# Keys and values of eight attention heads moved into the stage that multiplies with seven products, and its first products reordered

## The chip, the cores and the metric

The kernel runs on one core of one Trainium2 chip, in one launch. The metric is the device time of that core in microseconds (us), less is better. Engines are named as in the profile: PE is TensorE (PEld its weight load), DVE is VectorE, ACT is ScalarE, POOL is GpSimd, SP is SyncE, which issues all transfers here.

## The reference, cut to what matters

Two blocks run one after the other on a 1024 x 1024 activation (sequence by width). The change touches only the second one, after its state space branch:

```python
h = _rmsnorm(x, norm_w) * (1.0 + scale[:, None, :]) + shift[:, None, :]
proj = jnp.einsum("bsd,de->bse", h, w_in)
z_ssm, xbc, dt_raw, q, k, v, z_att, f_logit, g_logit = jnp.split(proj, offsets, axis=-1)
y_ssm = _ssd_branch(z_ssm, xbc, dt_raw, conv_w, conv_b, dt_bias, a_log, d_skip, ssm_norm_w)
y_att = _fox_branch(q, k, v, z_att, f_logit, b_f)
g_ssm, g_att = jnp.split(jax.nn.sigmoid(g_logit + b_gate), N_BRANCHES, axis=-1)
merged = g_ssm * jnp.einsum("bse,ed->bsd", y_ssm, w_proj_ssm) + g_att * jnp.einsum("bse,ed->bsd", y_att, w_proj_att)
...
# _fox_branch: eight heads of 128, causal, blocks of 128 queries
logits = jnp.einsum("bhqd,bhkd->bhqk", qi, k).astype(jnp.float32) * scale
logits = logits + fi[..., :, None] - f_cum[..., None, :]
logits = jnp.where(pi[:, None] >= kpos[None, :], logits, -jnp.inf)
probs = jax.nn.softmax(logits, axis=-1).astype(v.dtype)
return jnp.einsum("bhqk,bhkd->bhqd", probs, v)
```

So `q`, `k`, `v`, `z_att` and the gates are all products of the same `h` with columns of `w_in`, 128 columns for each head and each of `q`, `k`, `v`.

## The kernel before, in words

Everything is kept transposed: a tile has 128 features as partitions and the 1024 positions as columns, in two halves of 512. Float32 operands are split into a high part, rounded to the matmul's type, and a low part, the rest; a product takes three matmuls (high by high, high by low, low by high: `mm3`). `h` lies in SBUF split, as `Uh` and `Ul`.

**A block in the plain way** (`lin`) is 128 columns of weights by one half of 512 positions: 8 steps of 128 over the inner dimension of 1024, three matmuls each, 24 matmuls of 512 columns. A block has two halves. Its weights come by one transfer of 512 KB (`w_load`), ACT rounds them (`w_hi`, line 327), POOL subtracts (`w_lo`, line 334).

**The stage with seven products** (`stage_seven`) takes two blocks of weights at once, a pair. It treats the weights as 2 x 2 blocks (two blocks of columns by two halves of the inner dimension) and `h` as 2 x 2 (two halves of the inner dimension by two halves of positions) and forms the product with 7 multiplications in place of 8 (`PRODUCTS`: P1, P2, P7, P6, P4, P3, P5), of 12 matmuls each. So a pair takes 84 matmuls where the plain way takes 96. `SEVEN` lists the pairs, nine before: the attention's `z` (`fz`), seven of the gates `gs` and three of the gates `ga`. DVE adds weight blocks (`weight_add`), ACT and POOL split the sum (`weight_hi`, line 2684, `weight_lo`, line 2690) into one of four slots, DVE adds up the results from PSUM (`add`), ACT applies the gate, and SP stores the finished half in DRAM (`zd`, `md`, `gd`). `ORDER` is the order of the products. The sums of quadrants of `h` that P7, P6, P4 and P5 need (`quadrant`, `combine`, `x_hi`, `x_lo`) are made once, beside the first two pairs, and so the first 14 products are interleaved: P1, P2, P7 of pair 0, the same of pair 1, then P6, P4, P3, P5 of both.

**The attention** (`stage_attn_c`) is written as one loop over 64 steps, step i being block b = i % 8 (128 queries by (b + 1) x 128 keys) of head h = i // 8. In step i PE does, in this order: on odd steps the product of probabilities and values for two blocks (`values`), the transposes of block i - 3 (`turn_p`: as many as the block has key blocks, 1 to 8, line 3012), the scores of block i (`scores`), in steps 3 and 4 of a head the transposes of the values (`turn_v`), and then one piece of the projections of the **next** head (`head`): the two halves of `q` in steps 0 and 1, of `k` in 2 and 3, of `v` in 4 and 5, and a small one for the forget gate in 6 and 7. In head 7 steps 0 to 3 hold two blocks of `ga` instead and steps 4 to 7 hold nothing. Head 0's projections stand ahead of the loop.

What ties the engines together in a step: the transposed probabilities go to PSUM banks 4 and 5, one set for all blocks; ACT rounds them (line 3048), DVE takes the low part (line 3135), and only then may PE write the next transposes. The first `values` of a head waits for the low part of the transposed values (DVE, line 3157), which waits for ACT's rounding of them (line 3068).

The engines run their own queues in program order, and wait for each other by semaphores. The raw weights have two buffers, the halves of results of `stage_seven` six.

Of the kernel before, what the change touches and what calls it, by code (L numbers as in the profile page):

```python
# [11 lines left out]
P = 128  # L12
# [21 lines left out]
SEVEN = [(("fz", n), ("fz", n + 1)) for n in range(0, 8, 2)] + [(("gs", n), ("gs", n + 1)) for n in range(1, 7, 2)] + [  # L34
# [9 lines left out]
def weight_plan():  # L44
# [67 lines left out]
    first = {"fz": Z_ATT, "gs": G_LOG, "ga": G_LOG + 1024}  # L112
# [78 lines left out]
def program(nc, io, table):  # L191
    xT, pT, wflat, wada, vecs, rows, cst, abias, tabs, out = io
    stack = ExitStack()
    with stack:
# [50 lines left out]
        gd = nc.dram_tensor("gd", (8, P, T), F32, kind="Internal").ap()  # L245

# [2265 lines left out]
        def stage_ssm_out():  # L2512
# [70 lines left out]
            def gpsimd():  # L2583
# [7 lines left out]
                for n in range(8):  # L2591
                    w_lo(po, PSM[n] + 2)
                    if n == 6:
                        for x in range(2):
                            weight_lo(x)
                on.ends(po, "end ssm", "po")

            def sync():
                w_load(GS + 4)
                for n in range(8):  # L2600
                    w_load(PSM[n] + 4)
                    for hf in range(2):
# [31 lines left out]
        ORDER = [(p, q) for q in ("P1", "P2", "P7") for p in (0,)] + [(1, "P1"), (1, "P2"), (1, "P7")]  # L2634
        ORDER += [(p, q) for q in PRODUCTS[3:] for p in range(2)] + [(p, q) for p in range(2, len(SEVEN)) for q in PRODUCTS]
# [85 lines left out]
        def stage_seven():  # L2721
# [55 lines left out]
            def scalar():  # L2777
                for x in range(2, 4):
                    weight_hi(x)
                for j in range(2):  # L2780
                    x_hi("P6", j)
                    ac.activation(two(kept, j), two(fl["P6"], j), ACT.Copy).then_inc(*on.up(ac, "seven_ac/keep", j))
                for x, (p, q) in enumerate(ORDER):
# [4 lines left out]
                    if x == 1:  # L2788
                        for j in range(2):
                            x_hi("P4", j)  # L2790
                    if x == 4:
                        for j in range(2):
                            x_hi("P5", j)
# [6 lines left out]
            def add(p, q):  # L2800
                what = ps[:, bank[p, q], :]
                u, v_ = tile[p, 0, 1], tile[p, 1, 1]
                if q == "P1":
                    return
# [7 lines left out]
                elif q == "P6":  # L2812
# [5 lines left out]
                    dv.tensor_tensor(v_, ps[:, bank[p, "P7"], :], u, ALU.add).then_inc(*on.up(dv, "seven_dv/read", p, "P7"))  # L2818
                elif q == "P4":
# [5 lines left out]
                elif q == "P3":  # L2825
                    on.wait_ge(dv, "seven_dv/read", p, "P7")
                    dv.tensor_tensor(u, what, u, ALU.add).then_inc(*on.up(dv, "seven_dv/read", p, q))
                elif q == "P5":
# [4 lines left out]
                    on.ends(dv, "seven_dv/out", p, 0, 1)  # L2833

# [7 lines left out]
            def vector():  # L2842
                on.wait_ge(dv, "end ssm", "pe")
                for j in range(2):
# [4 lines left out]
                    combine("P6", j, fl["P6"], fh["P6"], ALU.add)  # L2849
                for x, (p, q) in enumerate(ORDER):  # L2850
                    if x + 5 < len(ORDER):
                        weight_add(*ORDER[x + 5])
                    if x == 0:
                        for j in range(2):
                            x_lo("P6", j)
                    add(p, q)
                    if x in (1, 4):
                        to = {1: "P4", 4: "P5"}[x]
                        for j in range(2):
                            quadrant((1, int(x == 4)), j, to, fl)  # L2860
# [18 lines left out]
            def sync():  # L2879
                pair_load(1)  # L2880
# [11 lines left out]
            def store(p, r, hf):  # L2892
                nm, n = SEVEN[p][r]
                on.wait_ge(sp, "seven_ac/gate", p, r, hf)
                if nm == "gs":
                    on.wait_ge(sp, "seven_dv/gated", p, r, hf)
                to = {"fz": zd, "gs": md, "ga": gd}[nm]
# [17 lines left out]
            return [stored[y][-1] for y in range(6)]  # L2915

        tiles_stored = stage_seven()
# [4 lines left out]
        Kf = [(Y([P, T], F32R), Y([P, T], F32R)) for _ in range(2)]  # L2922
        Vfh, Vfl = Y([P, 8, P], F32R), Y([P, 8, P], F32R)
# [10 lines left out]
        def stage_attn_c():  # L2934
            FQ, FK, FV, GA = BLK["fq"], BLK["fk"], BLK["fv"], BLK["ga"]
            NF = 64
            parts = [(FQ, 0), (FQ, 1), (FK, 0), (FK, 1), (FV, 0), (FV, 1), None, None]
# [41 lines left out]
            def head(h, s, b):  # L2979
                if parts[s]:  # L2980
                    W, hf = parts[s]
                    frees = {id(FQ): [("fq_lo", h, hf)], id(FK): [("fk_lo", h, hf)], id(FV): [("vf", h, hf)]}[id(W)]
                    bank[W[h], hf] = lin(W[h], hf, b, Uh, Ul, need_c, frees)
                else:
                    hf = s - 6
# [29 lines left out]
            def turn_v(h, c):  # L3015
                wait_bank(5)
                on.wait_ge(pe, "vf", h, c)
# [16 lines left out]
            def scalar():  # L3034
                for event in tiles_stored:
                    on.wait_ge(ac, *event)
                for s in range(8):
                    head_ac(0, s)
                    if s in (0, 2):
                        w_hi(parts[s][0][0] + 2)  # L3040
                w_hi(FV[0] + 2)
                for i in range(NF + 4):
# [15 lines left out]
                    if i and head_step(i - 1) and (i - 1) % 8 in (1, 3, 5):  # L3058

                        w_hi(parts[(i - 1) % 8][0][(i - 1) // 8 + 1] + 2)  # L3060
# [31 lines left out]
            def head_ac(h, s):  # L3092
                if parts[s]:
                    W, hf = parts[s]
# [386 lines left out]
```

## Time and profile before

| | |
|---|---|
| median of three runs | 2838.76 us (2838.16 to 2839.21) |
| the profiled execution | 2831.54 us, span 2830.2 us |
| PE busy, share of the span | 97% |
| DVE, ACT, POOL busy | 60%, 49%, 32% |
| chain that ended last | PE 89%, DVE 4%, ACT 3%, POOL 2% |
| PE's share of the chain in `mm3` (line 343) | 83% |
| HBM read, written | 139.10 MB, 26.21 MB |

The span is from the first to the last instruction of the profiled execution. A busy share is an average over stages with different limits; "idle before" in brackets in a row is the time an engine stood still ahead of the instruction, with what ended it. The seven-product stage runs from about 1954 us to 2141 us of the span, the attention from there to about 2640 us (with some blocks of `ga` at its end).

### The profile page before, as it was taken

Reading aid. Unit: us, or ns where it says so; the run is one execution under the profiler, and the core shown is the slowest. Engines: PE = TensorE matmul, PEld = TensorE weight load, DVE = VectorE, ACT = ScalarE, POOL = GpSimd, SP = SyncE. Lnnn points to the kernel's source line nnn. Section 1 sums busy time; section 2 is a strip of 40 time slices with the busy share of each in tenths; the row PEclk is TensorE's granted clock in tenths of the full one; section 3 lists DMA queues with packets and bytes.
Section 4 is the critical chain, followed back from the end, with each engine's and each line's share of the span. In section 5 each row is a group of like instructions: output and inputs, shape, how many; then the busy total and the mean of one; then the engine's idle time right before and its main releaser. Section 6 shows DMA issues by size and latency. Waiting matters only on the chain.

```text
span 2830.2 us, 36562 instructions
## 1 busy us (share of the span) xinstructions
PE 2737.2 (97%) x13692; PEld 2249.9 (79%) x13692; DVE 1684.0 (60%) x2861; ACT 1387.1 (49%) x2550; POOL 908.0 (32%) x745
## 2 busy tenths in 40 slices
PE   8999989999999999999998999998999999999997
PEld 6778867777788888887876777776787888888876
DVE  6667775643278888887557874556552444443344
ACT  5767863434266767675346335542432343334222
POOL 0334441223365655562122221123541111111431
PEclk9999999999999999999999999999999999999999
DMA  3111131221100000003211310033342110111242
GB/s 135 41 31 42 36 124 68 91 83 38 39 10 13 10 11 10 11 31 112 73 47 36 112 38 23 23 126 104 115 146 99 37 36 24 30 30 31 82 149 75
DMA packets 62367, 167.68 MB, mean 59 GB/s; under 512 B 7024, under 2 KB 15856, under 8 KB 61040
## 3 DMA queue, kind: packets, MB, share of 16 engines
q1 hardware_dynamic: 62192, 165.34, 17.7%
q8 instruction: 111, 1.82, 0.3%
q14 instruction: 64, 0.52, 0.1%
HBM read 139.10 MB, written 26.21 MB: 58 GB/s over the span
## 4 chain that ended last, share of the span: by engine, by line
PE 89%; DVE 4%; ACT 3%; POOL 2%; issue 2%; DMA 0%; POOLq 0%; ACTq 0%; DVEq 0%
PE ps L343 83%; PE ps L461 4%; PE ps L3012 1%; PE ps L787 1%; POOL t L1779 0%; POOL t L1327 0%; POOL t L1331 0%; ACT t L327 0%; DVE t L3370 0%; DMA t<-in_wflat 0%; DVE t L2337 0%; DVE t L1906 0%; DVE t L563 0%; ACT t L826 0%; POOL t L1329 0%
## 5 line engine op out<-in xcount | busy, mean ns | idle before, releaser
L343 PE MATMUL ps<-t,t 128*128 128x512 f32 (+8 forms) x11804 | 2579.0, 377 | 68.7 <-POOL t L2690 10.9
L343 PEld LDWEIGHTS ps<-t,t 128*128 128x128 f32 (+4 forms) x11804 | 2048.5, 185 | 528.9 <-issue 68.5
L334 POOL TENSOR_TENSOR t<-t,t 128x1024 fp32r<-128x1024 f32 (+2 forms) x151 | 322.6, 2137 | 1131.2 <-ACT t L327 769.4
L327 ACT ACTIVATE t<-t 128x1024 fp32r<-128x1024 f32 (+2 forms) x187 | 167.8, 898 | 437.5 <-PE ps L343 437.1
L1719 DVE TENSOR_TENSOR t<-ps,t 128x512 fp32r<-128x512 f32 x256 | 164.6, 684 | 33.3 <-ACT t L1627 31.2
L1779 POOL TENSOR_SCALAR t<-t,t 128x1024 f32<-128x1024 f32 x128 | 143.6, 1122 | 119.3 <-DVE t L1725 114.3
L461 PE MATMUL ps<-t,t 128*128 128x128 f32 x1176 | 157.4, 274 | 11.5 <-POOL t L1779 9.2
L461 PEld LDWEIGHTS ps<-t,t 128*128 128x128 f32 x1176 | 132.7, 141 | 30.2 <-issue 14.4
L1732 DVE TENSOR_REDUCE t<-ps 128x1 f32<-128x1024 f32 x128 | 154.2, 1204 | 0.5 <-PE ps L343 0.5
L1635 ACT ACTIVATE t<-ps,t 128x1024 f32<-128x1024 f32 x128 | 142.9, 1117 | 3.5 <-DVE t L1732 3.3
L1627 ACT ACTIVATE t<-ps 128x512 fp32r<-128x512 f32 x256 | 139.0, 591 | 9.4 <-PE ps L461 5.5
L2690 POOL TENSOR_TENSOR t<-t,t 128x512 fp32r<-128x512 f32 x63 | 90.1, 1436 | 89.0 <-ACT t L2684 89.0
L965 POOL TENSOR_SCALAR t<-t,t 128x384 f32<-128x384 f32 (+1 forms) x128 | 69.2, 560 | 129.1 <-DVE t L912 129.1
L1266 POOL TENSOR_TENSOR t<-t,t 128x512 f32<-128x512 f32 x31 | 49.6, 1600 | 147.3 <-DVE t L1175 147.3
L3135 DVE TENSOR_TENSOR t<-ps,t 128x128 fp32r<-128x128 f32 (+3 forms) x64 | 48.4, 756 | 74.8 <-ACT t L3048 74.7
L2684 ACT ACTIVATE t<-t 128x512 fp32r<-128x512 f32 x63 | 39.0, 627 | 79.7 <-PE ps L343 45.2
L826 ACT ACTIVATE t<-t,t 128x384 f32<-128x384 f32 (+1 forms) x128 | 73.8, 579 | 3.3 <-DVE t L896 2.8
L1327 POOL TENSOR_TENSOR t<-t,t 32x512 f32<-32x512 f32 x34 | 43.6, 1282 | 75.8 <-DVE t L1322 75.5
L3048 ACT ACTIVATE t<-ps 128x128 fp32r<-128x128 f32 (+3 forms) x64 | 41.7, 652 | 50.5 <-PE ps L3012 50.5
L2473 ACT ACTIVATE t<-ps,t 128x128 f32<-128x128 f32 x128 | 34.8, 383 | 60.1 <-PE ps L343 53.9
L887 DVE CUSTOM_DVE_ANT_0 t<-ps,t 128x384 f32<-128x384 f32 (+1 forms) x128 | 61.3, 519 | 4.1 <-PE ps L343 3.3
L334 DVE TENSOR_TENSOR t<-t,t 128x1024 fp32r<-128x1024 f32 (+1 forms) x36 | 31.6, 879 | 49.5 <-ACT t L327 49.5
(245 smaller groups left out, 2537.6 us busy)
## 6 DMA issues: line engine op xcount, KB each, us to landing
t<-in_wflat SPq DMA_DIRECT2D x138, 512.0 KB, 3.6
t<-in_wada SPq DMA_DIRECT2D x48, 256.0 KB, 4.9
t<-in_wflat SPq DMA_DIRECT2D x9, 1024.0 KB, 5.9
t<-in_xT SPq DMA_DIRECT2D x16, 512.0 KB, 7.2
md<-t SPq DMA_DIRECT2D x30, 256.0 KB, 3.2
t<-md SPq DMA_DIRECT2D x30, 256.0 KB, 4.0
t<-in_wflat SPq DMA_DIRECT2D x32, 128.0 KB, 2.0
hd<-t SPq DMA_DIRECT2D x8, 512.0 KB, 3.1
```

Source lines behind the costliest of these rows:

```text
L327: ac.activation(parts(i)[0][:, 0:n], raw[i % 2][:, 0:n], ACT.Copy).then_inc(*on.up(ac, "whi", i))
L334: e.tensor_tensor(lo[:, 0:n], raw[i % 2][:, 0:n], hi[:, 0:n], ALU.subtract) \
L343: return pe.matmul(o, l, r, start=start, stop=stop)
L461: t = pe.transpose(o[:, c * P:(c + 1) * P], src[:, c * P:(c + 1) * P], ident)
L826: ac.activation(S[:, r, 0:nk], S[:, r, 0:nk], ACT.Exp, bias=M[:, 8 + r:9 + r], accum_out=M[:, 16 + r:17 + r]) \
L965: po.tensor_scalar(S[:, r, 0:nk], S[:, r, 0:nk], M[:, 20 + r:21 + r], 1.0, ALU.mult, ALU.mult).then_inc(*on.up(po, "a probs", i, r))
L1627: ac.activation(to, src, ACT.Copy).then_inc(*on.up(ac, "b pT_hi", i - 3, c))
L1635: ac.activation(Pm[u][:, :], o, ACT.Exp, bias=bm[:, c0:c0 + 1], accum_out=bm[:, c0 + 1:c0 + 2]).then_inc(*on.up(ac, "b exp", i - 1))
L1719: dv.tensor_tensor(to, src, turned(i - 3, c, 0)[0], ALU.subtract).then_inc(*on.up(dv, "b pT_lo", i - 3, c))
L1732: dv.tensor_reduce(bm[:, c0:c0 + 1], o, AX, ALU.max, negate=True).then_inc(*on.up(dv, "b max", i))
L1779: po.tensor_scalar(Pm[u][:, :], Pm[u][:, :], bm[:, c0 + 2:c0 + 3], 1.0, ALU.mult, ALU.mult).then_inc(*on.up(po, "b probs", i - 1))
L2690: po.tensor_tensor(lo[:, :, :], weight(p, W_QUAD[q]), hi[:, :, :], ALU.subtract).then_inc(*on.up(po, "seven_po", p, q))
```

## The change

`SEVEN` gets eight more pairs at its front, (`fk`, h) with (`fv`, h): the keys and the values of head h. The blocks `fk` and `fv` leave the plain way. Their results go to two new DRAM tensors, `kd` and `vd`, without a gate, and come back in the attention by one transfer each per head (`key_load` into `Kraw`, which shares its place with the low part of the keys; `value_load` into `Vf`). ACT and DVE split the keys from SBUF instead of PSUM, and the copy of the values from PSUM by ACT goes away. In the attention, `q` of the next head stands in steps 0 and 3, the split of its keys in 1 and 2, and steps 4 and 5 have no projection.

`ORDER` puts P3 of pairs 0 and 1 directly behind their P7, and the DVE, ACT and SP code of the first 14 products is placed anew for it.

```diff
-SEVEN = [(("fz", n), ("fz", n + 1)) for n in range(0, 8, 2)] + ...
+SEVEN = [(("fk", h), ("fv", h)) for h in range(8)] + [(("fz", n), ("fz", n + 1)) for n in range(0, 8, 2)] + ...
...
     for h in range(8):
-        for nm, c in (("fq", Q_ATT), ("fk", K_ATT), ("fv", V_ATT)):
-            add(nm, W, None, 1024, (c + 128 * h, c + 128 * h + 128))
+        add("fq", W, None, 1024, (Q_ATT + 128 * h, Q_ATT + 128 * h + 128))
...
                 for n in range(8):
                     w_load(PSM[n] + 4)
+                    if n == 7:
+                        pair_load(1)
...
-        ORDER = [(p, q) for q in ("P1", "P2", "P7") for p in (0,)] + [(1, "P1"), (1, "P2"), (1, "P7")]
-        ORDER += [(p, q) for q in PRODUCTS[3:] for p in range(2)] + [(p, q) for p in range(2, len(SEVEN)) for q in PRODUCTS]
+        ORDER = [(p, q) for p in range(2) for q in ("P1", "P2", "P7", "P3")] + [(p, q) for q in ("P6", "P4", "P5") for p in range(2)]
+        ORDER += [(p, q) for p in range(2, len(SEVEN)) for q in PRODUCTS]
...
+                if nm in ("fk", "fv"):
+                    return
                 on.wait_ge(ac, "seven_dv/out", p, r, hf)
...
-                for x in range(2, 4):
-                    weight_hi(x)
+                weight_hi(2)
                 for j in range(2):
                     x_hi("P6", j)
                     ac.activation(two(kept, j), two(fl["P6"], j), ACT.Copy).then_inc(*on.up(ac, "seven_ac/keep", j))
+                    if j == 0:
+                        weight_hi(3)
...
-            parts = [(FQ, 0), (FQ, 1), (FK, 0), (FK, 1), (FV, 0), (FV, 1), None, None]
+            query = {0: 0, 3: 1}
+            key = {1: 0, 2: 1}
+            forget = {6: 0, 7: 1}
...
             def turn_v(h, c):
                 wait_bank(5)
-                on.wait_ge(pe, "vf", h, c)
+                on.wait_ge(pe, "m4", "v", h)
...
+                elif s in key:
+                    hf = key[s]
+                    for ev in slot_free(h):
+                        on.wait_ge(ac, *ev)
+                    on.wait_ge(ac, f"m{h % 2}", "k", h)
+                    ac.activation(Kf[h % 2][0][:, half(hf)], Kraw[h % 2][:, half(hf)], ACT.Copy).then_inc(*on.up(ac, "fk_hi", h, hf))
...
+            def key_load(h):
+                for ev in slot_free(h):
+                    on.wait_ge(sp, *ev)
+                for event in kept_at["fk", h]:
+                    on.wait_ge(sp, *event)
+                sp.dma_start(Kraw[h % 2][:, :], kd[h]).then_inc(*on.landed(sp, f"m{h % 2}", "k", h))
+
+            def value_load(h):
+                if h:
+                    on.wait_ge(sp, "c vT", h - 1, 1)
+                for event in kept_at["fv", h]:
+                    on.wait_ge(sp, *event)
+                sp.dma_start(Vf[:, :], vd[h]).then_inc(*on.landed(sp, "m4", "v", h))
```

Two places show what moves. The first is PE's queue in step 4 of head 0. In the kernel before it holds, after two transposes of probabilities, the scores of 640 keys, the transposes of the values' second half (line 461), and then a plain block. Of the two operands the moving one stands first: the keys (t_23367, t_23368) ahead of the queries, `h` (t_70, t_71) ahead of the block's weights (t_52, t_54):

```order
L3012 MATMUL ps<-t_55,t_23377 128x128 [waits s_probs_dv,s_pT_lo,s_pT_hi]
L3012 MATMUL ps<-t_55,t_23377 128x128
L343 MATMUL ps<-t_23367,t_23363 128x512 [waits s_fq_lo,s_max]
L343 MATMUL ps<-t_23368,t_23363 128x512
L343 MATMUL ps<-t_23367,t_23364 128x512
L343 MATMUL ps<-t_23367,t_23363 128x128
L343 MATMUL ps<-t_23368,t_23363 128x128
L343 MATMUL ps<-t_23367,t_23364 128x128
L343 MATMUL ps<-t_57,t_56 128x128
L461 MATMUL ps<-t_55,t_23378 128x128 [waits s_v_lo,s_v_hi]
L461 MATMUL ps<-t_55,t_23378 128x128 x3
L343 MATMUL ps<-t_70,t_52 128x512 [waits s_fk_lo,s_wlo_po,s_whi]
```

The same place in the changed kernel, from the scores of the last 128 keys on; t_24725 and t_24726 are the high and low part of the transposed probabilities, t_24723 and t_24724 those of the transposed values:

```order
L344 MATMUL ps<-t_24717,t_24714 128x128
L344 MATMUL ps<-t_57,t_56 128x128
L462 MATMUL ps<-t_55,t_24730 128x128 [waits s_v_lo,s_v_hi]
L462 MATMUL ps<-t_55,t_24730 128x128 x3
L344 MATMUL ps<-t_24725,t_24723 128x256 [waits s_v_lo,s_pT_lo,s_og]
L344 MATMUL ps<-t_24726,t_24723 128x256
L344 MATMUL ps<-t_24725,t_24724 128x256
```

Behind the transposes of the values there now stands at once the product with the values, which waits for their low part (s_v_lo); the 24 matmuls between the two are gone.

The second is ACT's queue at the start of the seven-product stage. t_20790, t_20792, t_20796 and t_20798 are the high parts of the four weight slots, t_20794 and t_20795 the raw weights of pairs 0 and 1, t_20778 and t_20781 the operand of P6 and its sum, t_20788 the copy that is kept. Before:

```order
L2684 ACTIVATE t_20796<-t_20794 128x512 [waits s_seven_dv]
L2684 ACTIVATE t_20798<-t_20795 128x512 [waits s_w71]
L2710 ACTIVATE t_20778<-t_20781 128x1024 [waits s_seven_dv]
L2782 ACTIVATE t_20788<-t_20781 128x1024
L2710 ACTIVATE t_20778<-t_20781 128x1024 [waits s_seven_dv]
L2782 ACTIVATE t_20788<-t_20781 128x1024
L2764 ACTIVATE t_63<-ps 128x512 [waits s_md2,s_md3,s_md1,s_ssm,s_md0,s_mm]
```

And in the changed kernel:

```order
L2688 ACTIVATE t_20796<-t_20794 128x512 [waits s_seven_dv]
L2714 ACTIVATE t_20778<-t_20781 128x1024 [waits s_seven_dv]
L2787 ACTIVATE t_20788<-t_20781 128x1024
L2688 ACTIVATE t_20798<-t_20794 128x512 [waits s_seven_dv]
L2714 ACTIVATE t_20778<-t_20781 128x1024 [waits s_seven_dv]
L2787 ACTIVATE t_20788<-t_20781 128x1024
L2768 ACTIVATE t_63<-ps 128x512 [waits s_md2,s_md3,s_md1,s_ssm,s_md0,s_mm]
L2688 ACTIVATE t_20790<-t_20795 128x512 [waits s_w71]
```

The fourth slot now takes a block of pair 0 (P3) and waits for DVE, not for the transfer of pair 1 (s_w71); the first weights of pair 1 have moved behind both halves of P6's operand and the first copy out of PSUM (line 2768).

## Rows read from the trace of the kernel before

**Rows 1.** Windows (us): busy time (x count) by engine, granted PE clock, DMA share, GB/s.

```profile
1955.00:1990.00 35.00, 24.09 (x85) 18.20 (x85) 29.57 (x23) 13.56 (x18) 15.25 (x8) 0.85 0.22 82
2180.00:2560.00 380.00, 379.27 (x2056) 321.57 (x2055) 159.61 (x408) 145.41 (x304) 51.34 (x22) 1.00 0.13 42
2580.00:2593.00 13.00, 10.00 (x66) 8.54 (x64) 8.83 (x23) 7.39 (x14) 2.37 (x1) 1.00 0.14 42
```

**Rows 2.** Timeline of DVE, end of the seven-product stage (start us, us, what).

```profile
2127.77 0.69 DVE L2810 TENSOR_TENSOR t<-ps,t 128x512 f32<-128x512 f32 x1 [2.11 <-PE ps L343]
...
2141.37 0.69 DVE L2830 TENSOR_TENSOR t<-ps,t 128x512 f32<-128x512 f32 x1 [2.03 <-PE ps L343]
```

**Rows 3.** Timeline of ACT, plain blocks of head 0 ahead of the loop.

```profile
2147.05 0.60 ACT L3105 ACTIVATE t<-ps 128x512 fp32r<-128x512 f32 x1 [3.62 <-PE ps L343]
...
2174.96 0.60 ACT L3100 ACTIVATE t<-ps 128x512 f32<-128x512 f32 x1 [5.00 <-PE ps L343]
```

**Rows 4.** Timeline of PE, one middle head of the attention.

```profile
2357.51 0.30 PE L3012 MATMUL ps<-t,t 128*128 128x128 f32 x1
...
2364.45 0.38 PE L3012 MATMUL ps<-t,t 128*128 128x128 f32 x2
...
2385.59 0.84 PE L3012 MATMUL ps<-t,t 128*128 128x128 f32 x6
...
2394.69 0.95 PE L3012 MATMUL ps<-t,t 128*128 128x128 f32 x7
...
2401.55 1.04 PE L3012 MATMUL ps<-t,t 128*128 128x128 f32 x8
2402.34 9.28 PE L343 MATMUL ps<-t,t 128*128 128x384 f32 x52
2411.45 0.30 PE L3012 MATMUL ps<-t,t 128*128 128x128 f32 x1
```

**Rows 5.** Timeline, head 7, steps 4 to the end of 7.

```profile
2580.20 0.38 PE L3012 MATMUL ps<-t,t 128*128 128x128 f32 x2
...
2583.53 0.69 DVE L3157 TENSOR_TENSOR t<-ps,t 128x512 fp32r<-128x512 f32 x1 [0.19 <-ACT t L3068]
2584.37 0.88 PE L343 MATMUL ps<-t,t 128*128 128x256 f32 x6 [2.23 <-DVE t L3157]
...
2593.18 0.85 PE L3012 MATMUL ps<-t,t 128*128 128x128 f32 x6 [0.26 <-issue]
```

**Rows 6.** Timeline, the last transposes of the attention and what follows on ACT and DVE.

```profile
2601.53 0.95 PE L3012 MATMUL ps<-t,t 128*128 128x128 f32 x7
...
2602.51 0.92 ACT L3048 ACTIVATE t<-ps 128x896 fp32r<-128x896 f32 x1 [6.52 <-PE ps L3012]
2603.47 1.09 DVE L3135 TENSOR_TENSOR t<-ps,t 128x896 fp32r<-128x896 f32 x1 [1.32 <-ACT t L3048]
...
2609.14 1.01 ACT L3048 ACTIVATE t<-ps 128x1024 fp32r<-128x1024 f32 x1
...
2610.18 1.23 DVE L3135 TENSOR_TENSOR t<-ps,t 128x1024 fp32r<-128x1024 f32 x1 [5.62 <-ACT t L3048]
```

**Rows 7.** Waits of PE: total us, times, longest.

```profile
PE ps L343 <- POOL t L2690: 10.9, 4, 5.0
```

**Rows 8.** Timeline, start of the seven-product stage.

```profile
1959.28 0.49 SPq L2645 DMA_DIRECT2D t<-in_wflat  x1
...
1966.16 0.63 ACT L2684 ACTIVATE t<-t 128x512 fp32r<-128x512 f32 x1 [10.67 <-DMA t<-in_wflat]
...
1968.19 4.61 PE L343 MATMUL ps<-t,t 128*128 128x512 f32 x12 [4.98 <-POOL t L2690]
...
1983.54 16.81 PE L343 MATMUL ps<-t,t 128*128 128x512 f32 x62 [4.71 <-POOL t L2690]
```

**Rows 9.** DMA issues of the page: count, KB each, us to landing.

```profile
t<-in_wflat SPq DMA_DIRECT2D x138, 512.0 KB, 3.6
...
t<-in_wflat SPq DMA_DIRECT2D x9, 1024.0 KB, 5.9
```

More of the change, by code:

```diff
@@ L31 @@
 X_ORDER = [0, 1, 2, 3, 8, 9, 4, 5, 6, 7]
-SEVEN = [(("fz", n), ("fz", n + 1)) for n in range(0, 8, 2)] + [(("gs", n), ("gs", n + 1)) for n in range(1, 7, 2)] + [
+SEVEN = [(("fk", h), ("fv", h)) for h in range(8)] + [(("fz", n), ("fz", n + 1)) for n in range(0, 8, 2)] + [(("gs", n), ("gs", n + 1)) for n in range(1, 7, 2)] + [
     (("gs", 7), ("ga", 5)), (("ga", 6), ("ga", 7))]
@@ L2787, in scalar @@
                         weight_hi(x + 4)
-                    if x == 1:
+                    if x in (3, 6):
                         for j in range(2):
[L2790 to L2793, printed above, removed]
+                            x_hi("P4" if x == 3 else "P5", j)
                     for _, p_, r, hf in [o for o in outs if o[0] == x - 1]:
@@ L2802, in add @@
                 u, v_ = tile[p, 0, 1], tile[p, 1, 1]
-                if q == "P1":
+                if q == "P1" or q == "P3" and p < 2:
                     return
@@ L2818, in add @@
                     dv.tensor_tensor(v_, ps[:, bank[p, "P7"], :], u, ALU.add).then_inc(*on.up(dv, "seven_dv/read", p, "P7"))
+                    if p < 2:
+                        third(p)
                 elif q == "P4":
@@ L2825, in add @@
                 elif q == "P3":
-                    on.wait_ge(dv, "seven_dv/read", p, "P7")
-                    dv.tensor_tensor(u, what, u, ALU.add).then_inc(*on.up(dv, "seven_dv/read", p, q))
+                    third(p)
                 elif q == "P5":
@@ L2833, in add, with third @@
                     on.ends(dv, "seven_dv/out", p, 0, 1)
+            def third(p):
+                u = tile[p, 0, 1]
+                on.wait_ge(dv, "mm/seven", p, "P3")
+                on.wait_ge(dv, "seven_dv/read", p, "P7")
+                dv.tensor_tensor(u, ps[:, bank[p, "P3"], :], u, ALU.add).then_inc(*on.up(dv, "seven_dv/read", p, "P3"))
             def scale(p, r, hf):
@@ L2893, in store @@
                 nm, n = SEVEN[p][r]
-                on.wait_ge(sp, "seven_ac/gate", p, r, hf)
+                if nm in ("fk", "fv"):
+                    on.wait_ge(sp, "seven_dv/out", p, r, hf)
+                else:
+                    on.wait_ge(sp, "seven_ac/gate", p, r, hf)
                 if nm == "gs":
                     on.wait_ge(sp, "seven_dv/gated", p, r, hf)
-                to = {"fz": zd, "gs": md, "ga": gd}[nm]
+                to = {"fk": kd, "fv": vd, "fz": zd, "gs": md, "ga": gd}[nm]
                 sp.dma_start(to[n, :, half(hf)], tile[p, r, hf]).then_inc(*on.landed(sp, f"pt{store_of[p, r, hf]}", p, r, hf))
@@ L2914, in stage_seven @@
             sync()
-            return [stored[y][-1] for y in range(6)]
-        tiles_stored = stage_seven()
+            kept_at = {SEVEN[p][r]: [(f"pt{store_of[p, r, hf]}", p, r, hf) for hf in range(2)] for p in range(len(SEVEN)) for r in range(2)}
+            return [stored[y][-1] for y in range(6)], kept_at
+        tiles_stored, kept_at = stage_seven()
         Y = region(YO)
@@ L2922, in program @@
         Kf = [(Y([P, T], F32R), Y([P, T], F32R)) for _ in range(2)]
+        Kraw = [at(YO + 16384 + 8192 * x + 4096, [P, T]) for x in range(2)]
         Vfh, Vfl = Y([P, 8, P], F32R), Y([P, 8, P], F32R)
@@ L2979, in head @@
             def head(h, s, b):
[L2980 to L2985, printed above, removed]
+                if s in query:
+                    hf = query[s]
+                    bank[FQ[h], hf] = lin(FQ[h], hf, b, Uh, Ul, need_c, [("fq_lo", h, hf)])
+                elif s in forget:
+                    hf = forget[s]
                     bank["f", h, hf] = b
@@ L3038, in scalar @@
                     head_ac(0, s)
[L3039 to L3041 removed]
+                    if s == 3:
+                        w_hi(FQ[0] + 2)
                 for i in range(NF + 4):
@@ L3057, in scalar @@
                             .then_inc(*on.up(ac, "c exp", i - 1))
-                    if i and head_step(i - 1) and (i - 1) % 8 in (1, 3, 5):
-                        w_hi(parts[(i - 1) % 8][0][(i - 1) // 8 + 1] + 2)
+                    if i and head_step(i - 1) and (i - 1) % 8 == 3:
+                        w_hi(FQ[(i - 1) // 8 + 1] + 2)
                     if i in (NF - 6, NF - 4):
```

99 lines of the change are left out of this document (52 added, 47 removed).

## The prediction

> **What bounds the kernel now.** I read the windows first, then PE's own timeline, then who waited. The windows show that the attention is bound by PE: of 380 us PE is busy for 379.27, DVE for 159.61, ACT for 145.41 [rows 1]. A matmul taken out there shortens the run for as long as PE stays the engine that is never waited for. The seven-product stage has PE waits only at its start: four, 10.9 us together, all for POOL's low weight parts [rows 7]; at the full rate of its steady part it waits for nothing.
>
> Then the price of the two ways to compute a block. In the steady part of the seven-product stage DVE is released by the end of a product at 2127.77 and at 2141.37, five products later: 2.72 us a product [rows 2]. In the plain way ACT is released at 2147.05 and at 2174.96, five half blocks later: 5.58 us each [rows 3]. A pair costs 7 x 2.72 = 19.0 us one way and 4 x 5.58 = 22.3 us the other.
>
> Third, what the plain blocks hide. A middle head takes PE from 2357.51 to 2411.45 (one transpose to the next single transpose), 53.9 us, with no idle time [rows 4]; six half blocks are 33.5 of them. In head 7, steps 4 to 7 have no block behind them, and there PE does stand still: 2.23 us for the low part of the values on DVE, itself released by ACT [rows 5]. The changed kernel makes that the state of every head.
>
> **The change, part by part.**
>
> *Products added.* 8 pairs x 7 = 56 products x 2.72 = +152.3 us. The added pairs need no gate on ACT, DVE's and POOL's work per pair is as before, and PE waited for none of them in the steady part.
>
> *Half blocks removed.* 8 heads x 4 = 32 x 5.58 = -178.6 us, if PE never waits. Together -26.3 us. That is what the edit gives on paper.
>
> *Cover lost in steps 4 to 7, heads 0 to 6.* From the two transposes of step 4 to the six of the next step 0 a middle head takes 2385.59 - 2364.45 = 21.14 us [rows 4]. Two half blocks less: 9.98. Head 7 does the same work without blocks, and takes 2593.18 - 2580.20 = 12.98 [rows 5]. So 3.0 us are waits. Two small matmuls for the forget gate come on top in heads 0 to 6; they partly fall into the waits, so I take 3.2 (bounds 2.3, the one named wait, and 3.6). What is late: step 4 transposes the values, ACT takes them behind a transposed block, an exponential and a rounding of weights, DVE behind that, and the product with the values stands right behind it in PE's queue (first place of the queues above). 7 x 3.2 = +22.4 us.
>
> *Cover lost in steps 1 and 2, heads 1 to 6.* Before, the seven transposes of step 1, the eight of step 2 and the product with the values in step 3 each had a half block between them. All transposes share banks 4 and 5, so the next may start only when ACT and DVE have read the last. The last head shows the pieces. Seven transposes: 0.95 on PE, 0.92 on ACT, 1.09 on DVE, with the hops between them 3.07 us until the eight may start. Eight: 1.04 + 1.01 + 1.23, with hops 3.4 until the product with the values may start [rows 4, 6]. That product and what goes with it take 9.11 (2402.34 to 2411.45) less a half block of 5.58 less the scores, 0.58 (three matmuls of 384 columns at 5.58 / 24 per 512, and the mask) = 2.95 [rows 4]. In all 3.07 + 3.41 + 2.95 = 9.4 us from the seven transposes to the single one. PE's own work there is 2411.45 - 2394.69 = 16.76 less two half blocks = 5.6. So 3.8 us of waits (bounds 3.3 and 4.4 for the hops), x 6 = +23 us. The split of the keys, now from SBUF, stands behind the transposed block on ACT and DVE, and delays neither.
>
> *Start of the attention.* Head 0 loses the cover in steps 1 and 2 too, where its first transpose waits for the first exponential, and ACT takes a rounding of weights ahead of the forget gate. No row has it; it lies between nothing and the half block that hid it, 5.6. I take +3.
>
> *First keys and values.* A reload of 512 KB takes 3.6 us to land [rows 9]. It is issued when the scores of the head before last in that buffer are done (end of step 7) and read in step 1 of the next head, with a half block of 5.58 and 3 us of other PE work between: hidden. Without that cover it would cost up to 3.6 us a head.
>
> *Reordered first products.* PE waits 4.98 us ahead of 1968.19 for pair 1, whose transfer is issued at 1959.28 and lands by 1966.16, and 4.71 us ahead of 1983.54 [rows 8]. P3 of pair 0 needs no transfer and fills 2.7 us of the first wait; P3 of pair 1 fills the same of the second. The slow clock goes too: the 12 matmuls at 1968.19 take 4.61 us instead of 2.72, the 62 at 1983.54 take 16.81 instead of 14.1, and the clock of the stretch is 0.85 [rows 1, 8]. Against it: pair 1's first weights stand on ACT behind both halves of P6's operand (second place of the queues), about a product later; and pair 2's transfer, 5.9 us [rows 9], starts after P5 of pair 0 as before, while the 14 products now end sooner, so PE may wait for it. I take -6 us, between 0 and -15 (all of the waits and some 4 us of slow clock).
>
> **The sum**: -26.3 + 22.4 + 23 + 3 - 6 = +16 us. The profiled execution took 2831.54, so 2847.6 in its terms; the median of the runs lies 7.2 above it, so I forecast 2838.8 + 16 = 2855 us, +0.57%.
>
> **The rivals.**
>
> *PE's clock falls in every head* (slower by far). After a wait of 5 us the 12 matmuls took 4.61 us [rows 8]. Were it so after the waits of each head, two groups of that size at 1.9 us for 7 heads would add 27 us: 2882. Against it: head 7 has 3 us of idle time in 13 at a granted clock of 1.00, 2.4 GHz [rows 1], and the new waits are no longer, 1.8 to 2.5 us, though they recur. The Trainium skill ("TensorE: Matmul & The Clock Gate", HAM oscillation) describes a loop in which every round waits, the clock falls in the wait, and each round starts at the low rate. By that rule the time would be the 2882; by head 7's row it stays at the forecast. 8%.
>
> *The second pair of waits isn't there* (faster). If the transposes of steps 1 and 2 did not bind, 23 us go: -7, 2832. The place is the read of banks 4 and 5 by line 3135. It decides where waits in the attention fall below 32 us in all. For it speaks only that no row has such a wait, as a block always covered it; against it the durations in [rows 6], each measured. 9%.
>
> *Waits a third smaller, or all of the start's 15 us recovered*: within 0.2% of before, 2835 to 2844. 9%.
>
> *Reloads late*: SP's queue is one, and a key transfer stands behind weights and the `z` tiles. 7 heads x 2 us: 2869. 5%.
>
> *The start gives nothing*, since the weights only wait elsewhere: 2861 to 2864. 7%.
>
> The forecast's own case, 2846 to 2862, gets 62%.
>
> **How the numbers follow.** 0.2%, 5.7 us, is about what a measurement of this kernel can tell from no change. Slower: 62 + 8 + 5 + 7 = 82%; same 9; faster 9. The bounds of the terms give 7 x 2.3 + 6 x 3.3 - 15 - 26.3 = -5 at one end and 7 x 3.6 + 6 x 4.4 + 5.6 - 26.3 = +31 at the other; the range from 2839 to 2869 leaves out the faster case below and the clock above.
>
> **What would show it.** In the changed profile: the seven-product stage is longer by 152 less some 6 us, with 2.7 us a product; PE's waits at its start fall from 10.9 to about 5. A middle head takes 53.9 - 22.3 + 7.0 = 38.6 us from single transpose to single transpose. PE waits on the values' low part (line 3157 before) some 2.3 us in seven heads more, and on the transposed low part (line 3135 before) some 3.8 us a head. The clock in the attention stays 1.00. It is wrong if a head takes near 32 us (no waits) or over 42 (clock or reloads), or if the stage's start grows.

## The result, and the profile after

The changed kernel takes 2870.41 us (median of 4 runs, 2864.94 to 2872.38), the kernel before 2838.66 us on the same chip (4 runs, 2838.16 to 2839.21). The ratio is 1.0115, 95% interval 1.0101 to 1.0129: slower, as forecast, but 15 us above the forecast of 2855 and just outside the range that ended at 2869. The profiled execution took 2868.45 us with a span of 2867.0, the one before 2831.54 with 2830.2. Between the profiles lie 36.8 us of span, between the medians 31.8; the sum of the prediction was +16. The account below goes by the profiles, so it has 20.8 us to explain, and not the 15.4 of the medians.

The page's first part for the kernel after, and the first line of its fourth (the chain that ended last, by engine):

```profile
PE 2728.9 (95%) x13596; PEld 2243.1 (78%) x13596; DVE 1752.4 (61%) x2949; ACT 1404.0 (49%) x2582; POOL 955.5 (33%) x785
...
PE 86%; DVE 6%; ACT 3%; issue 2%; POOL 2%; DMA 0%; POOLq 0%; ACTq 0%; DVEq 0%
```

PE falls from 97% of the span to 95%, and DVE's share of the chain rises from 4% to 6%: PE now stands waiting for DVE. The waits of PE say where (total us, times, longest). Only those of the two stages that the change touches stand here:

```profile
PE ps L344 <- DVE t L3178: 17.5, 8, 2.2
PE ps L344 <- DVE t L3156: 13.0, 12, 1.9
PE ps L3037 <- issue: 10.8, 7, 1.8
...
PE ps L344 <- POOL t L2694: 7.7, 5, 2.9
...
PE ps L344 <- DVE t L2822: 7.0, 1, 7.0
...
PE ps L3037 <- DVE t L3174: 2.0, 1, 2.0
```

Line 3178 takes the low part of the transposed values, line 3156 that of the transposed probabilities (3157 and 3135 before); line 3037 is the transpose. The wait put down to "issue" is that of the eight transposes: they start at 2399.22, right behind the end of the low part of the seven, which reads the same banks 4 and 5:

```profile
2398.03 1.09 DVE L3156 TENSOR_TENSOR t<-ps,t 128x896 fp32r<-128x896 f32 x1 [1.31 <-ACT t L3072]
```

These three waits make 41 us; before, the first two of them made 2.8 us, in head 7 alone [rows 5]. The start's wait on POOL went down from 10.9 [rows 7] to 7.7, but one of 7.0 us for line 2822 is new.

PE's timeline, two middle heads in a row, from single transpose to single transpose (start us, us, what; in brackets the idle time before and what ended it):

```profile
2367.13 0.30 PE L3037 MATMUL ps<-t,t 128*128 128x128 f32 x1
...
2374.06 0.38 PE L3037 MATMUL ps<-t,t 128*128 128x128 f32 x2
...
2378.18 0.88 PE L344 MATMUL ps<-t,t 128*128 128x256 f32 x6 [2.19 <-DVE t L3178]
...
2383.12 1.59 PE L344 MATMUL ps<-t,t 128*128 128x256 f32 x12 [0.29 <-DVE t L3156]
...
2386.98 0.85 PE L3037 MATMUL ps<-t,t 128*128 128x128 f32 x6
...
2396.08 0.95 PE L3037 MATMUL ps<-t,t 128*128 128x128 f32 x7
...
2399.22 1.06 PE L3037 MATMUL ps<-t,t 128*128 128x128 f32 x8 [1.76 <-issue]
...
2402.75 4.49 PE L344 MATMUL ps<-t,t 128*128 128x256 f32 x24 [1.88 <-DVE t L3156]
2407.03 0.37 PE L3037 MATMUL ps<-t,t 128*128 128x128 f32 x1
...
2439.22 1.06 PE L3037 MATMUL ps<-t,t 128*128 128x128 f32 x8 [1.76 <-issue]
...
2442.74 3.04 PE L344 MATMUL ps<-t,t 128*128 128x256 f32 x24 [1.88 <-DVE t L3156]
2445.62 0.30 PE L3037 MATMUL ps<-t,t 128*128 128x128 f32 x1
```

The second head takes 2445.62 - 2407.03 = 38.59 us, the forecast's 38.6. The first takes 39.90 with the very same waits: the 24 matmuls of the values' product take 4.49 instead of 3.04 us. The windows of three heads give the reason in the third value from the row's end, the granted clock (the DMA share and GB/s stand behind it). The first of them goes from step 3 of head 0 to step 3 of head 1:

```profile
2324.78:2367.13 42.35, 36.41 (x198) 31.94 (x199) 24.54 (x64) 18.54 (x42) 2.37 (x1) 0.88 0.21 78
2367.13:2407.03 39.90, 33.57 (x200) 29.27 (x200) 22.71 (x58) 17.59 (x39) 2.38 (x1) 0.96 0.12 40
2407.03:2445.62 38.59, 32.24 (x200) 27.95 (x201) 22.72 (x58) 17.58 (x39) 2.38 (x1) 1.00 0.13 42
```

Within the first middle head the clock is down only behind the second pair of waits, at 2399.22 and 2402.75. Through the wait of 2.19 us at 2378.18 it stays at 1.00 (2374.00 to 2387.00):

```profile
2380.00:2390.00 10.00, 9.49 (x59) 8.05 (x58) 8.93 (x21) 8.09 (x19) 0.00 (x0) 1.00 0.33 105
2390.00:2400.00 10.00, 8.24 (x54) 7.29 (x53) 4.08 (x14) 2.44 (x6) 0.00 (x0) 1.00 0.01 2
2400.00:2410.00 10.00, 8.12 (x47) 7.53 (x46) 5.96 (x17) 3.50 (x8) 0.00 (x0) 0.83 0.00 1
```

The start of the seven-product stage on PE, and then DVE there:

```profile
1962.66 3.01 PE L344 MATMUL ps<-t,t 128*128 128x512 f32 x12 [0.91 <-POOL t L2694]
1968.59 3.06 PE L344 MATMUL ps<-t,t 128*128 128x512 f32 x12 [2.92 <-POOL t L2694]
1974.17 9.80 PE L344 MATMUL ps<-t,t 128*128 128x512 f32 x36 [2.52 <-POOL t L2694]
1984.97 3.02 PE L344 MATMUL ps<-t,t 128*128 128x512 f32 x12 [0.99 <-POOL t L2694]
1988.34 5.78 PE L344 MATMUL ps<-t,t 128*128 128x512 f32 x24 [0.35 <-POOL t L2694]
2001.12 9.05 PE L344 MATMUL ps<-t,t 128*128 128x512 f32 x32 [7.00 <-DVE t L2822]
```

```profile
1995.02 1.29 DVE L2673 TENSOR_TENSOR t<-t 128x512 f32<-128x512 f32 x2
1996.22 3.42 DVE L2720 TENSOR_TENSOR t<-t,t 128x1024 fp32r<-128x1024 f32 x2
1999.57 0.68 DVE L2818 TENSOR_TENSOR t<-ps,t 128x512 f32<-128x512 f32 x1
2000.28 0.69 DVE L2822 TENSOR_TENSOR t<-ps,t 128x512 f32<-128x512 f32 x1
```

The products go round the eight PSUM banks. The eleventh, P4 of pair 0, writes the bank of the third, P7 of pair 0. That bank is read by line 2822, which comes behind P6's add; and ahead of P6's add DVE has the weight sums and the low part of P5's operand (line 2720, 3.42 us). PE is released when line 2822 has read, at 2000.97. The banks are taken in turn, so it doesn't help that those of P1 and P2 of pair 1 have been read by then. In the order before, P6 of pair 0 was the seventh product and its adds stood ahead of that work.

**The account, by stretches.** Each starts and ends with an instruction that both kernels have. The ends of before are those of its own trace ([rows 2] has the last product's read at 2141.37). First the ends that no row has shown yet, before and after:

```profile
1960.19 3.01 PE L343 MATMUL ps<-t,t 128*128 128x512 f32 x12 [0.91 <-POOL t L2690]
2195.73 0.27 PE L3012 MATMUL ps<-t,t 128*128 128x128 f32 x1
2573.27 0.30 PE L3012 MATMUL ps<-t,t 128*128 128x128 f32 x1
```

```profile
2299.43 0.69 DVE L2835 TENSOR_TENSOR t<-ps,t 128x512 f32<-128x512 f32 x1 [2.03 <-PE ps L344]
2324.78 0.33 PE L3037 MATMUL ps<-t,t 128*128 128x128 f32 x1 [1.97 <-DVE t L3174]
2609.80 0.30 PE L3037 MATMUL ps<-t,t 128*128 128x128 f32 x1
```

| stretch | before | after | difference | forecast |
|---|---|---|---|---|
| start of the span to P7 of pair 0 | 1960.19 | 1962.66 | +2.5 | 0 |
| to the last product's read (2141.37; 2299.43) | 181.18 | 336.77 | +155.6 | +146.3 |
| to the single transpose in step 3 of head 0 | 54.36 | 25.35 | -29.0 | -30.5 |
| seven heads, to that of head 7 | 377.54 | 285.02 | -92.5 | -99.7 |
| to the end | 256.9 | 257.2 | +0.3 | 0 |

The forecast column is the terms of the sum laid on these stretches: 152.3 - 6; six half blocks and +3; 26 half blocks, 22.4 and 23. The miss of 20.8 us is 9.3 in the start, 7.2 in the seven heads, 2.5 ahead of P7 of pair 0, 1.5 at the attention's start, and 0.3 at the end.

### The profile page after: what moved, and what is told of

Read it like the earlier page. It is cut to its first block, busy times and chain, and to the rows that moved or that the text cites. A ratio compares the mean times of both kernels' runs of the same rounds, so it can differ in the third digit from the quotient of the medians.

```text
span 2867.0 us, 36671 instructions
## 1 busy us (share of the span) xinstructions
PE 2728.9 (95%) x13596; PEld 2243.1 (78%) x13596; DVE 1752.4 (61%) x2949; ACT 1404.0 (49%) x2582; POOL 955.5 (33%) x785
## 4 chain that ended last, share of the span: by engine, by line
PE 86%; DVE 6%; ACT 3%; issue 2%; POOL 2%; DMA 0%; POOLq 0%; ACTq 0%; DVEq 0%
PE ps L344 80%; PE ps L462 4%; PE ps L3037 1%; PE ps L788 1%; DVE t L3156 1%; ACT t L328 1%; POOL t L1780 0%; POOL t L1328 0%; POOL t L1332 0%; ACT t L3072 0%; DVE t L2709 0%; DVE t L3165 0%; DVE t L3409 0%; DVE t L2703 0%; DVE t L888 0%
## 5 line engine op out<-in xcount | busy, mean ns | idle before, releaser
L344 PEld LDWEIGHTS ps<-t,t 128*128 128x128 f32 (+3 forms) x11708 | 2041.9, 186 | 560.0 <-issue 98.6
L335 POOL TENSOR_TENSOR t<-t,t 128x1024 fp32r<-128x1024 f32 (+2 forms) x135 | 284.3, 2106 | 1050.6 <-ACT t L328 752.3
L328 ACT ACTIVATE t<-t 128x1024 fp32r<-128x1024 f32 (+2 forms) x171 | 151.1, 883 | 425.7 <-PE ps L344 425.6
L2694 POOL TENSOR_TENSOR t<-t,t 128x512 fp32r<-128x512 f32 x119 | 174.5, 1469 | 160.2 <-ACT t L2688 160.2
L2688 ACT ACTIVATE t<-t 128x512 fp32r<-128x512 f32 x119 | 74.5, 631 | 180.5 <-PE ps L344 130.0
L462 PEld LDWEIGHTS ps<-t,t 128*128 128x128 f32 x1176 | 133.1, 141 | 30.5 <-issue 14.6
L335 DVE TENSOR_TENSOR t<-t,t 128x1024 fp32r<-128x1024 f32 (+1 forms) x36 | 31.6, 878 | 48.7 <-ACT t L328 48.7
```

The lines of the kernel that those rows point to most:

```text
L328: ac.activation(parts(i)[0][:, 0:n], raw[i % 2][:, 0:n], ACT.Copy).then_inc(*on.up(ac, "whi", i))
L335: e.tensor_tensor(lo[:, 0:n], raw[i % 2][:, 0:n], hi[:, 0:n], ALU.subtract) \
L344: return pe.matmul(o, l, r, start=start, stop=stop)
L462: t = pe.transpose(o[:, c * P:(c + 1) * P], src[:, c * P:(c + 1) * P], ident)
L2688: ac.activation(slots[x % 4][0][:, :, :], weight(p, W_QUAD[q]), ACT.Copy).then_inc(*on.up(ac, "seven_ac/w", p, q))
L2694: po.tensor_tensor(lo[:, :, :], weight(p, W_QUAD[q]), hi[:, :, :], ALU.subtract).then_inc(*on.up(po, "seven_po", p, q))
```

## The experiments

Two questions were open: is the start's +9.3 the bank of P7, or something the eight added pairs do; and is the seven heads' loss a matter of the waits alone, or of the clock? All times are against the kernel before on the same chip: 2833.09 us there (15 runs) for the first, second and fourth experiment, 2832.83 us (7 runs) for the others. The changed kernel itself was timed only beside the kernel before at 2838.66 us, so an experiment is compared with it by the two ratios or, better, by stretches of the traces. The ratios are estimated from all the runs and can differ a little from the quotient of the medians. Every edit is to the changed kernel, where nothing else is said.

### The reordered start alone

The kernel before, with the first 14 products in the new order and their ACT, DVE, POOL and SP code, and nothing else of the change.

```diff
-        ORDER = [(p, q) for q in ("P1", "P2", "P7") for p in (0,)] + [(1, "P1"), (1, "P2"), (1, "P7")]
-        ORDER += [(p, q) for q in PRODUCTS[3:] for p in range(2)] + [(p, q) for p in range(2, len(SEVEN)) for q in PRODUCTS]
+        ORDER = [(p, q) for p in range(2) for q in ("P1", "P2", "P7", "P3")] + [(p, q) for q in ("P6", "P4", "P5") for p in range(2)]
+        ORDER += [(p, q) for p in range(2, len(SEVEN)) for q in PRODUCTS]
```

> The kernel before with only the reordered first 14 products (nine pairs as before). Theory A: 2838.7 + 3 = 2842 us, with a wait of PE of 5 to 7 us for the add of P7's result. Rival B: 2833 us, no such wait. If the wait depends on the gates that the first pairs have here and the new ones have not, it is longer than 7 us.

Measured: 2841.12 us (10 runs), ratio 1.0022 (1.0010 to 1.0034). The waits of PE in its trace:

```profile
PE ps L343 <- POOL t L2693: 7.7, 5, 2.9
...
PE ps L343 <- DVE t L2819: 7.1, 1, 7.1
```

They are the changed kernel's waits, without the new pairs. From P7 of pair 0 to the last product's read it takes 2150.65 - 1966.20 = 184.45 us, against 181.18 before: +3.3 where the sum had -6. The reorder by itself costs time. The medians differ by 8.0 us, the stretch by 3.3. The ten times lie in two groups: three from 2832.59 to 2836.62 at a mean granted clock of 0.991 to 0.994, and seven from 2841.06 to 2845.65 at 0.989 to 0.990. The profiled one is of the second group, and in it P7 of pair 0 starts 6.0 us later than in the profile of before; that part is taken up below.

### The low part of P5's operand later

DVE takes it behind the adds that free the banks of pair 0 and 1.

```diff
-                    if x in (0, 4, 7):
+                    if x in (0, 4, 10):
                         for j in range(2):
-                            x_lo({0: "P6", 4: "P4", 7: "P5"}[x], j)
+                            x_lo({0: "P6", 4: "P4", 10: "P5"}[x], j)
```

> The changed kernel with one edit: DVE makes the low part of P5's operand (two instructions, 3.4 us) after the adds of P6's results, not before. Theory A: the ninth to eleventh products wait for the PSUM bank of P7, which those adds free; the 7.0 us wait falls by 3.4 us and the time to 2867 us. Rival: P5's own operand is then late and the wait moves there; no change from 2870 us.

Measured: 2862.74 us (4 runs), ratio 1.0106 (1.0091 to 1.0122). PE at the eleventh product:

```profile
1994.77 7.56 PE L344 MATMUL ps<-t,t 128*128 128x512 f32 x25 [3.69 <-DVE t L2822]
```

The wait falls by 3.3 us, from 7.00 to 3.69, near the 3.42 us of the two instructions that moved, and no wait for P5's operand comes in its place. The stretch falls from 336.77 to 2293.17 - 1959.66 = 333.51. So DVE's queue ahead of line 2822 is what PE waited for. Of the other 3.7 us nothing was tried; P5's operand sums and the weight sums still stand ahead there. The ratios, 1.0106 and 1.0115, are too near to tell apart; it is the stretch that shows the gain.

### The old start, with the new pairs

The changed kernel with the first 14 products and their code as before; the lines of the first diff backwards.

> The changed kernel with the eight new pairs, but the first 14 products of the seven-product stage in the order and code of before. From P7 of pair 0 to the last product the stage took 181.2 us before, 184.5 us with the reordered start alone and 336.8 us in the changed kernel. Theory A (the reordered start costs 3.3 us, with or without the new pairs): here that stretch takes 333.5 us, and the time is 3 us under the changed kernel's, ratio to before near 1.010. Rival B (the prediction, the reordering gains 6 us): 343 us, ratio 1.0135.

Measured: 2863.93 us (4 runs), ratio 1.0100 (1.0081 to 1.0120). The stretch takes 2293.20 - 1959.78 = 333.42 us, 3.35 less than in the changed kernel. Its waits on POOL are those of before, and none is for a bank:

```profile
PE ps L344 <- POOL t L2691: 10.7, 4, 4.8
```

The eight pairs alone thus cost 333.42 - 181.18 = 152.24 us: the 152.3 of the sum. They add nothing to the start. The time is again told by the stretch: the ratios of 1.0100 and 1.0115 have intervals that overlap.

### The queries' blocks spread over the waits

After the change each head has two half blocks left, for the queries of the next head, in steps 0 and 3, where PE needs no cover. They are cut into pieces of 3 to 15 matmuls and put where PE waits. ACT's and DVE's parts of the queries move a step later.

```diff
-            query = {0: 0, 3: 1}
+            query = {2: 0, 4: 1}
+            pieces = {0: [(0, 0, 3)], 1: [(0, 3, 6)], 2: [(0, 6, None), (1, 0, 1)], 3: [(1, 1, 3)], 4: [(1, 3, None)]}
...
-                if s in query:
+                if h and s in pieces:
+                    for hf, k0, k1 in pieces[s]:
+                        bank[FQ[h], hf] = lin(FQ[h], hf, (7, 3)[hf], Uh, Ul, need_c, [("fq_lo", h, hf)], None, k0, k1)
+                elif s in query:
```

> The changed kernel with the two half blocks of q of the next head cut into pieces of 9 to 15 matmuls behind steps 0, 1, 2 and 4 of a head (6 in step 3), where PE waits, instead of whole blocks in steps 0 and 3. Same work. Theory A (the waits are latency of single chains, each 2 to 3 us, that any matmul can cover): a middle head falls from 39.9 us to 31.6 to 33, and the time by 7 x 7 to 7 x 8 us, to 2815 to 2823 us, below the kernel before. Rival (DVE and ACT are too far behind in a head as a whole, so that waits only move): a head stays above 36 us and the time above 2845 us.

Measured: 2824.45 us (6 runs), ratio 0.9964 (0.9952 to 0.9976): faster than before, though the start still has its 7.0 us wait. It is just above the 2815 to 2823 us expected. A middle head (line 3198 takes the low part of the queries, line 3160 that of the transposed probabilities):

```profile
2359.91 0.30 PE L3041 MATMUL ps<-t,t 128*128 128x128 f32 x1
...
2369.59 1.34 PE L344 MATMUL ps<-t,t 128*128 128x512 f32 x7 [0.53 <-DVE t L3198]
...
2373.53 1.59 PE L344 MATMUL ps<-t,t 128*128 128x256 f32 x12 [0.59 <-DVE t L3160]
...
2392.77 0.30 PE L3041 MATMUL ps<-t,t 128*128 128x128 f32 x1
```

32.86 us, where 53.94 less four half blocks of 5.58 is 31.6. The same matmuls, in another order, take 5.7 us a head less than in the 38.59 us head. All but 1.2 us of a head's loss was cover that was missing, and nothing else that the change brought: the reloads and the split from SBUF are still there.

### Both: spread blocks and the old start

> Both mended: the pieces of q behind the steps where PE waits (as in the run before) and the old start. Theory: the two are additive, the head at 32.9 us and the stretch at 333.5 us; 3.3 us less than the spread pieces alone, ratio to before near 0.995. Rival: the gain of the start is lost in the attention, ratio 0.9964 as before.

Measured: 2818.06 us (4 runs), ratio 0.9939 (0.9920 to 0.9958). The interval touches that of the spread pieces alone, so the traces must tell. From P7 of pair 0 to the last product's read it takes 2298.66 - 1965.43 = 333.23 us, where the spread pieces alone take 2303.12 - 1966.45 = 336.67, and the heads take 32.8: the two gains add up. It is the fastest kernel here that does all the work, and brings in 14.8 us of the 26.3 on paper.

### Useless matmuls in the waits

The changed kernel with 7, 7 and 9 extra matmuls of 512 columns behind steps 1, 2 and 4 of each head, whose result nobody reads. It does more work than the changed kernel; what it takes away is only that PE stands still.

```diff
                         head(*head_step(i), (7, 1, 7, 3, 7, 5, 7, 7)[i % 8])
+                        if i % 8 in (1, 2, 4):
+                            fill({1: 7, 2: 7, 4: 9}[i % 8])
...
+            def fill(n):
+                wait_bank(7)
+                for _ in range(n):
+                    mm(ps[:, 7, :], idr[:, :], Uh[:, 0, half(0)], True, True)
```

> The changed kernel with 7, 7 and 9 useless matmuls of 512 columns behind steps 1, 2 and 4 of heads 0 to 6, written to a bank that nobody reads: PE is busy in place of waiting, all other work is the same. Theory A (some 1.3 us a head are matmuls at the low clock behind the waits): the product with the values in step 3 takes 3.0 us again in place of 4.4 to 4.5, a middle head falls from 39.9 to about 38.7 us, and the time by 6 to 9 us; the granted clock in the attention is 1.00. Rival (the matmuls are slow for another reason, or the low clock costs nothing on the path): the head stays at 39.9 us or grows.

Measured: 2860.18 us (4 runs), ratio 1.0088 (1.0071 to 1.0104). The end of a middle head:

```profile
2399.92 3.04 PE L344 MATMUL ps<-t,t 128*128 128x256 f32 x24 [0.21 <-DVE t L3163]
2402.80 0.30 PE L3044 MATMUL ps<-t,t 128*128 128x128 f32 x1
```

and five heads in one window, first of the changed kernel, then of this one:

```profile
2350.00:2550.00 200.00, 168.31 (x1004) 146.23 (x1004) 114.67 (x295) 87.94 (x196) 11.90 (x5) 0.97 0.12 40
```

```profile
2350.00:2550.00 200.00, 195.62 (x1154) 165.89 (x1152) 115.47 (x293) 90.25 (x200) 11.94 (x5) 1.00 0.13 40
```

Every middle head now takes 38.5 us (2364.29, 2402.80, 2441.29), and the values' product 3.04. The seven heads take 2602.43 - 2325.82 = 276.61 us, against 285.02 in the changed kernel, whose other instructions are the same: with more matmuls 8.4 us less, at a clock of 1.00 instead of 0.97. This is the price of the clock in that trace, and 276.61 lies 1.2 us below the 377.54 - 99.7 = 277.8 of the forecast.

### Thin keys and values in the kernel before

The kernel before, where the keys' and values' blocks of heads 1 to 7 do 3 of their 24 matmuls, the rest left out. No new pairs, no reloads, no transfers changed. There is one run of it.

```diff
-                    bank[W[h], hf] = lin(W[h], hf, b, Uh, Ul, need_c, frees)
+                    bank[W[h], hf] = lin(W[h], hf, b, Uh, Ul, need_c, frees) if W is FQ or not h else thin(W[h], hf, b, frees)
```

> The kernel before with the projections of k and v of heads 1 to 7 cut to 3 matmuls of their 24 (one eighth of the inner dimension; the rest is left out), nothing else changed: no new pairs, no reloads, keys split from PSUM. It takes 28 x 21 x 0.2325 = 137 us of PE work out of the attention. Theory A (lost cover is what made PE wait, whatever the keys come from): a middle head takes 38 us or more instead of 53.94 - 4 x 4.88 = 34.4, with waits for the low parts of the values and of the transposed probabilities, and the profiled time is 2720 to 2730 us. Rival (the waits come from the reloads or the split from SBUF): the head takes 34.4 us, the time 2695 us.

Measured: 2719.32 us. Middle heads take 37.56 us (2268.10 to 2305.63 to 2343.19), 3.1 more than the 34.4 that the matmuls left need (53.94 less four times 21 of 24 parts of 5.58), with these waits:

```profile
PE ps L343 <- DVE t L3166: 13.7, 8, 2.2
...
PE ps L343 <- DVE t L3144: 7.7, 7, 1.1
```

They are the waits for the values' low part and the transposed low part again. Both numbers lie just under what was expected of my theory (38 and more, 2720 to 2730), since each thin block still covers a little and the queries' blocks stand in steps 0 and 1 here. That reason is not tested. They are far from the 34.4 and 2695 of the rival. Taking the matmuls away is enough to make the waits. The values' product takes 3.03 us here and the clock from 2350 to 2450 us is 1.00: behind waits of 1.6 and 1.1 us it did not fall.

## Why the prediction was right about the sign and short by 15 us

**The two prices held.** The old start with the new pairs shows 152.24 us for the 56 products (sum: 152.3). The half blocks were 5.58 each: the spread kernel's head of 32.86 less its waits of 0.53 and 0.59 is 31.7, where 53.94 less four half blocks is 31.6.

**Cover lost in steps 4 to 7: right.** From the two transposes of step 4 to the six of the next step 0 the changed kernel takes 2386.98 - 2374.06 = 12.92 us, with a wait of 2.19 for the values' low part and 0.29 behind it. The forecast had 9.98 + 3.2 = 13.2, from head 7 [rows 5].

**Cover lost in steps 1 and 2: right.** From the seven transposes to the eight 3.14 us (3.07), on to the values' product 3.53 (3.41), and from there to the single transpose 2445.62 - 2442.74 = 2.88 (2.95). Together 9.55 against 9.43. The chain of small durations on PE, ACT and DVE, with the hops between them [rows 6], gave a wait that no row of before showed. The rival in which these waits were absent falls.

**Reloads of keys and values: hidden, right.** At the first keys, ACT waits for a transfer once, on a place that PE does not feel:

```profile
2306.59 1.16 ACT L3128 ACTIVATE t<-t 128x512 fp32r<-128x512 f32 x2 [0.88 <-DMA t<-kd]
```

**The reordered first products: the step that failed.** The sum said "I take -6 us, between 0 and -15"; the runs show +3.3. Part of the argument came true: the wait on POOL fell by 3.2 us, from 10.9 to 7.7 and not to about 5, and the 12 matmuls behind the longest of these waits take 3.06 us, not 4.61. P3 of pair 0 "needs no transfer", but its weights are a sum that DVE makes, and it waits 2.92 us for their low part itself. Little of the slow clock was saved: behind the new wait it is 0.67 from 2001.12 to 2006.12. The waits together rise by 3.8 us and the stretch by 3.3. Without the bank's wait of 7.0 it would be some 3.7 us shorter than before, an estimate from these two numbers; no run shows it.

What turned the gain into a loss is the bank: the step looked at what PE's next operand waits for, and never at what its next bank waits for. P3 of two pairs put early means that two more banks are filled before the first read of P7's, while DVE's queue kept P5's operand ahead of that read. The step's own bounds excluded a loss, with no reason given for it. The reordered start alone shows the 3.3 us as a loss and the old start as a gain of 3.35. The later low part shows that the bank's wait hangs on DVE's queue.

**The clock: a rival that came true in part.** "PE's clock falls in every head" was given 8% and a price of 27 us, 1.9 for each of two groups of 12 matmuls a head. (The 1.9 is 4.61 less 2.72, the steady distance of two products; a group of 12 at the full clock has 3.01 in the row of 1960.19, so the same row gives 1.6.) What happened costs 8.4 us in seven heads: 3.9 in the first, where the starting waits of the attention stand close together and the clock is 0.88, and 1.4 in three of the others, where some of the 24 matmuls behind the waits of 1.76 and 1.88 us ran at the low one of the two levels, 1.2 GHz; three stayed at 1.00. The claim "The clock in the attention stays 1.00" rested on head 7 with 3 us of idle time in 13 [rows 1]. That row showed the waits of steps 4 to 7. It did not show the second pair of waits with 1.65 us of work between them (2399.22 to 2400.87), and in the middle heads the drop stands only behind that pair. So the sum had a term at nothing that measured 8.4 us. The Trainium skill ("TensorE: Matmul & The Clock Gate", HAM oscillation) describes a loop whose waits let the clock fall so that each round starts at the low rate; the trace agrees in kind, and differs in that only some rounds do. By the sum: 1.2 us fewer for the waits, 8.4 more for the clock, +7.2.

**Start of the attention: +3 taken, +4.5 measured,** within its bounds of 0 and 5.6. PE waits 1.18 us for the queries' low part, 1.49 for the forget gate on ACT, and 1.97 for the first probabilities. A part of it is the clock again: it is 0.93 in this stretch of 25.35 us, and where it is 1.00, in the old start's trace, the same stretch takes 2317.01 - 2293.20 = 23.81 us, which makes the term +2.9.

**The rest, 2.5 us ahead of the stage, doesn't follow the change.** P7 of pair 0 starts at 1960.19 before. With the old order of the first products it starts at 1959.78 (old start) and 1965.43 (both); with the new one at 1959.66 (low part later), 1960.94 (useless matmuls), 1962.66 (changed kernel), 1966.20 (start alone) and 1966.45 (spread blocks). The granted clock from 1400 to 1950 us goes with it: 0.98 in the four that start behind 1962, 0.99 in the four that start ahead of 1961. What makes the clock differ there stays open. A difference of less than some 7 us between two profiles' totals therefore says nothing, and stretches must be compared. In medians the change costs 31.8 us, 5 less than in the two profiles: the median lies 7.2 us above the profiled execution before, and 2.0 after. Nothing run here says which stretch has those 5.

## What to carry to other kernels

A matmul that is removed gives back its time only if PE had nothing to wait for behind it: before taking work off the engine that bounds the kernel, lay the chain of the other engines (transpose, copy, low part) against what PE has left in that place, and move what is left to where the waits will be. The same two half blocks a head, cut up, turned a loss of 1.2% into a gain of 0.4%. When products are reordered that go round the PSUM banks, ask of each who reads the bank it takes over, and what stands ahead of that read in DVE's queue.

## What was not expected of the hardware

Behind two waits under 2 us each, 1.76 and 1.88 with 1.65 us of work between, TensorE's granted clock fell in some heads and not in others, in turn: 39.90, 38.59, 39.87, 38.56, 39.87 us. The waits are the same in all five, so they alone don't decide it, and what does stays open. Behind the wait of 2.19 us in the middle heads, with 0.29 as the next one, and behind 1.6 and 1.1 us, it did not fall. Adding 23 useless matmuls to each head took 8.4 us off the seven heads. The whole kernel's ratios to before, 1.0088 and 1.0115, have intervals that overlap, so it is the stretch in the traces that shows it.
